# Norms by a diagonal matrix of inverse roots on TensorE, with weight and shift applied in the evictions and the residual in pieces

## The chip, the cores and the metric

The kernel runs on one core of a Trainium2 chip. The metric is the device time of one execution in microseconds (us). The core has TensorE (PE, with PEld for its weight loads), VectorE (DVE), ScalarE (ACT), GpSimd (POOL) and a queue of transfers issued by SyncE (SP). ACT and POOL issue transfers too.

## The reference, cut to what matters

Two transformer stacks follow each other, all in float32. The first has two layers on 256 rows of 1024 numbers; the second has two layers on the same rows and 256 context rows.

```
def rms_norm(x, g):            # over 1024 numbers of a row
    return x * rsqrt(mean(x*x) + 1e-6) * g
# first stack, l = 0, 1
x = x + 0.5 * swiglu_ffn(rms_norm(x, ffn1_norm[l]), ...)          # norms 0, 4
h = rms_norm(x, mix_norm[l]); u = h @ w_in[l]                     # norms 1, 5
x = x + concat(conv, pool, attention of u) @ w_out[l]
x = x + 0.5 * swiglu_ffn(rms_norm(x, ffn2_norm[l]), ...)          # norms 2, 6
x = rms_norm(x, post_norm[l])                                     # norms 3, 7
# second stack, for latent rows xl and context rows xc
h = rms_norm(x, g) * (1 + scale) + shift                          # norms 8, 9, 10, 11
x = x + gate * mixer(h);  x = x + gate * experts(h)
```

Norm 8 feeds the first mixer (Fourier and short convolution), 9 and 11 the two mixtures of 32 experts, 10 the window attention. The last mixer and mixture give latent rows only, so norm 11 has 256 rows.

## The kernel before

Rows lie in four tiles of 128 (`xres`, partitions = rows): tiles 0 and 1 are the latent rows, 2 and 3 the context rows. Norms 0 to 7 and 11 have 2 tiles, 8 to 10 have 4. All large products run in TensorE as three products of a high and a low part (`product`: hi*hi, hi*lo, lo*hi). Weights come in panels of 1 MB, read by SP into four raw slots; `split(p)` makes the high part on ACT (a cast, L1128) and the low part on DVE (L1537, helper `rest`), in three slots. Each engine runs its own list of instructions in program order; they meet at semaphores.

A norm is `norm(n)` on DVE (L1583) and ACT (L1151), `norm_T(n)` on PE (L627) and `hT_rest(n)` on DVE (L1609). After the last panel of a stage, `residual` adds the product in PSUM (the banks that TensorE writes) to `xres`, 2 tiles of 1024 columns, and only then counts `x_ready`. Half of the tiles are squared and summed on DVE (L1586), half on ACT (L1160). ACT takes the square root (L1163), DVE inverts it and refines it with one Newton step (L1565 to L1554), then multiplies each row by root and weight into `hrow` (L1603). With modulation it is root times weight times (1 + scale) (L1599), and then plus shift (L1601). PE transposes 128x128 blocks of `hrow` with the identity (L634, transpose mode), 8 blocks a tile, four to a bank. ACT casts each bank into `t_hi` (L1170), DVE writes the rest into `t_lo`. PE starts its next product when all of it is there.

Norms 3 and 7 (`post_norm`) write `xres` itself, and norm 4 or 8 follows in full. `gated_residual` (L1800) does the same as `residual` with a gate row, tile after tile. After the experts, DVE combines four tiles (L2050 to L2054), and norm 10 follows. In norms 9 and 11 the rows `hrow` also go to DRAM, where the experts' rows are gathered from; the weights of the experts are then streamed. SP loads the expert panels 4 and 5 after `row_ready`.

The order within `moe`, `even` and `odd` is written out by hand. `norm_rows(n)` on ACT issues the loads of weight, scale and shift rows, each copied over all 128 partitions; `ffn` on DVE and ACT goes through 11 units of three panels.

Of the kernel before, what the change touches and what calls it, by code (L numbers as in the profile page):

```python
# [22 lines left out]
ALU = mybir.AluOpType  # L23
# [96 lines left out]
def build(nc, A, out):  # L120
# [11 lines left out]
    with ExitStack() as ctx:  # L132
# [23 lines left out]
        eps = sb("eps", [P, 1])  # L156
        ss = sb("sum_squares", [P, 64])
# [26 lines left out]


# [25 lines left out]
        cols1 = sb("cols1", [P, DEPTH, 2 * CONV_W + 8])  # L211
# [106 lines left out]
        ms_ready = sem("mean_square_ready")  # L318
        std_ready = sem("std_ready")
# [106 lines left out]
        gain_src = []  # L426
        for l in range(DEPTH):
            gain_src += [A["ffn1_norm"][l], A["mix_norm"][l], A["ffn2_norm"][l], A["post_norm"][l]]
        for l in range(DEPTH):
            gain_src += [A["norm_mix_g_2"][l], A["norm_ffn_g_2"][l]]  # L430


        MODB = [16 * c for c in (5, 10, 15, 18)]
# [51 lines left out]
        def _(sp):  # L485
# [57 lines left out]
            def moe(m):  # L543
# [12 lines left out]
                def first_load(x, src):  # L556
                    if x < RAW:
                        sp.wait_ge(w_ready, SPLIT_PANELS[m] + x - RAW + 1)
                    else:
                        sp.wait_ge(row_ready, TILE0[10 + 2 * m])  # L560
# [56 lines left out]
        def _(pe):  # L617
# [9 lines left out]
            def norm_T(n):  # L627

                nt = NORMS[n]
                pe.wait_ge(row_ready, TILE0[n + 1])  # L630
                for j in range(2 * nt):
                    for q in range(4):
                        kk, t = (2 * j + q // 2, q % 2) if nt == 2 else (j, q)
                        mm = pe.transpose(ps[:, j, q * P:(q + 1) * P], hrow[:, t, kk * P:(kk + 1) * P], ident)  # L634
                    mm.then_inc(tr_ready, 1)

# [22 lines left out]
            def ffn(f, n):  # L659
                p0 = G0[f"ffn{f}"]  # L660
                pe.wait_ge(hT_lo, BANK0[n + 1])
                pe.wait_ge(cond_ready, 1)

                def gate_up(u, j, par, mk=None):

                    for half in range(2):
# [5 lines left out]
                        for c in range(2):  # L672
                            for kk in range(KD):
                                mm = product(ps[:, 4 + 2 * par + c, half * PC:(half + 1) * PC],
# [4 lines left out]
                def ffn_down(u, p, j, par, start=False, stop=False):  # L679
# [4 lines left out]
                    for c in range(2):  # L684
                        for t in range(2):
                            for half in range(2):
                                mm = product(ps[:, 2 * t + half, :], T(AT + (2 * par + c) * 256 + t * P, P),
                                             at(wt, slice(None), c, slice(half * BANK, (half + 1) * BANK)),
                                             start and c == 0, stop and c == 1)
# [13 lines left out]
                ffn_down(10, p0 + 32, 32, 0, stop=True)  # L703

            def mix1(l):
# [3 lines left out]
                pe.wait_ge(hT_lo, BANK0[n + 1])  # L709
# [3 lines left out]
                for b in range(2):  # L713
                    pe.wait_ge(w_ready, p + b + 1)
                    for c in range(2):
                        for kk in range(KD):
                            mm = product(ps[:, b, c * 256:(c + 1) * 256],
# [106 lines left out]
                for q in range(4):  # L824
                    rows_product(G0[f"out{l}"] + q, lambda kk, t: T(2048 + kk * 256 + t * P, P), 2,
                                 lambda t: ps[:, 2 * t + q // 2, (q % 2) * 256:(q % 2) * 256 + 256])
# [12 lines left out]
            def even():  # L839
                p = G0["even"]  # L840
                norm_T(8)
                pe.wait_ge(hT_lo, BANK0[9])
                for half in range(2):
                    rows_product(p + half, hT4, 4, lambda t: ps[:, t, half * 256:half * 256 + 256])
# [45 lines left out]
                for q in range(4):  # L890
                    rows_product(G0["even_out"] + q, lambda kk, t: T(kk * 512 + t * P, P),
                                 4, lambda t: ps[:, 2 * t + q // 2, (q % 2) * 256:(q % 2) * 256 + 256])

            def moe(m):
                nt, n = TILES[m], 9 + 2 * m
                nb, b0 = BLOCKS[m], EXPERTS * m
                norm_T(n)
                pe.wait_ge(hT_lo, BANK0[n + 1])
# [3 lines left out]
                for t in range(nt):  # L902
                    for kk in range(KD):
                        for part in range(2):
                            mm = pe.matmul(ps[:, 0, 2 * t * NLOG:2 * (t + 1) * NLOG], lhs(kk, t)[part],
                                           router_split(kk), start=kk == 0 and part == 0,
                                           stop=kk == KD - 1 and part == 1)
# [205 lines left out]
        def _(act):  # L1113
# [37 lines left out]
            def norm(n, mid=None):  # L1151
# [5 lines left out]
                if n:  # L1157
                    act.wait_ge(x_ready, n)
# [1136 lines left out]
```

## Time and profile before

| | |
|---|---|
| median of 3 runs | 2908.72 us (2908.54 to 2909.84) |
| profiled execution, its own time | 2905.86 us |
| its span, first to last instruction | 2904.0 us |
| mean granted clock of TensorE | 0.900 |
| busy: PE, PEld, DVE, ACT, POOL | 2310.4, 1590.7, 1070.7, 686.9, 117.8 us |

A busy share is an average over stages: the two expert stages (roughly 1440 to 2035 and 2310 to 2890 us) wait for transfers, the others run on PE. A timeline row gives the start, the length, the engine, line and operation, what it writes and reads, and in brackets the idle time ahead of it with what ended it.

### The profile page before, as it was taken

How to read it: one execution, taken by the hardware profiler on the slowest of the kernel's cores; microseconds unless marked ns; L12 is line 12 of the kernel's file. 1: busy time of each engine (PE TensorE's matmuls, PEld its weight loads, DVE VectorE, ACT ScalarE, POOL GpSimd, SP SyncE). 2: the span in 40 equal slices, each digit the busy share in tenths (PEclk: the TensorE clock that was granted, in tenths of full speed). 3: DMA queues.
4: the chain of work that ended last, by engine and by line, in shares of the span. 5: the costliest groups of instructions: out<-in, count | busy, mean ns of one | idle time of the engine just before them, and what ended most of it. 6: DMA issues, size and time to landing. Idle time of an engine off the chain costs nothing.

```text
span 2904.0 us, 35200 instructions
## 1 busy us (share of the span) xinstructions
PE 2310.4 (80%) x13750; PEld 1590.7 (55%) x13750; DVE 1070.7 (37%) x1570; ACT 686.9 (24%) x876; POOL 117.8 (4%) x209
## 2 busy tenths in 40 slices
PE   5998679979987699699558777877369668888885
PEld 5888478878885688587523333332355523333332
DVE  4555545555556355723420100010668410000011
ACT  3334433333335233321101000100335200000100
POOL 0001000000010000000000000000100000000000
PEclk9999789989998799899669999999679788998898
DMA  7775137757752287422149999999420269999997
GB/s 260 261 238 173 56 118 266 253 190 266 262 169 88 104 288 259 139 78 94 73 161 401 399 396 400 402 400 404 179 71 1 87 258 397 401 399 401 401 402 303
DMA packets 242628, 718.82 MB, mean 248 GB/s; under 512 B 17040, under 2 KB 156560, under 8 KB 189072
## 3 DMA queue, kind: packets, MB, share of 16 engines
q1 hardware_dynamic: 213584, 642.82, 59.7%
q10 hardware_dynamic: 19952, 48.45, 4.6%
q0 software_dynamic: 8976, 25.90, 3.0%
q8 instruction: 87, 1.43, 0.2%
q14 instruction: 29, 0.24, 0.0%
HBM read 693.70 MB, written 25.26 MB: 248 GB/s over the span
## 4 chain that ended last, share of the span: by engine, by line
PE 55%; DMA 26%; DVE 9%; issue 4%; DVEq 2%; ACT 2%; SPq 1%; ACTq 0%; POOL 0%; POOLq 0%
DMA raw<-in_w 24%; PE ps L620 13%; PE ps L621 12%; PE ps L622 12%; PE ps L934 10%; PE ps L655 2%; PE ps L634 1%; SPq L554 1%; PE ps L936 1%; PE ps L1071 1%; DVE t_lo L1537 1%; PE ps L1086 1%; DMA raw<-in_ffn_w_up 1%; DVE work L1601 1%; DMA work<-expert_rows,slot_of_token 1%
## 5 line engine op out<-in xcount | busy, mean ns | idle before, releaser
L1537 DVE TENSOR_TENSOR w_lo<-raw,w_hi 128x2048 fp32r<-128x2048 f32 x180 | 411.4, 2290 | 445.1 <-ACT w_hi L1128 445.1
L620 PE MATMUL ps<-t_hi,w_hi 128*128 128x256 f32 (+1 forms) x1568 | 456.4, 291 | 8.7 <-DVE t_lo L1537 8.6
L621 PE MATMUL ps<-t_lo,w_hi 128*128 128x256 f32 (+1 forms) x1568 | 454.1, 290 | 0.0
L622 PE MATMUL ps<-t_hi,w_lo 128*128 128x256 f32 (+1 forms) x1568 | 451.1, 288 | 0.0
L1128 ACT CAST w_hi<-raw 128x2048 fp32r<-128x2048 f32 x180 | 342.1, 1903 | 447.5 <-PE ps L622 428.5
L934 PE MATMUL ps<-raw,work 128*64 128x512 f32 x528 | 308.8, 742 | 167.0 <-DMA raw<-in_w 165.6
L2015 DVE COPY work<-ps 128x512 f32<-128x512 f32 x64 | 44.3, 692 | 932.6 <-PE ps L952 932.6
L620 PE MATMUL ps<-w_hi,t_hi 128*128 128x256 f32 (+1 forms) x1088 | 349.8, 322 | 15.3 <-DVE t_lo L1537 12.4
L622 PE MATMUL ps<-w_hi,t_lo 128*128 128x256 f32 (+1 forms) x1088 | 351.1, 323 | 0.0
L621 PE MATMUL ps<-w_lo,t_hi 128*128 128x256 f32 (+1 forms) x1088 | 351.0, 323 | 0.0
L620 PEld LDWEIGHTS ps<-t_hi,w_hi 128*128 128x128 f32 x1568 | 296.6, 189 | 30.4 <-issue 13.2
L936 PE MATMUL ps<-raw,work 128*64 128x512 f32 x528 | 310.5, 745 | 0.0
L622 PEld LDWEIGHTS ps<-t_hi,w_lo 128*128 128x128 f32 x1568 | 297.6, 190 | 4.6
L621 PEld LDWEIGHTS ps<-t_lo,w_hi 128*128 128x128 f32 x1568 | 296.1, 189 | 5.6
L934 PEld LDWEIGHTS ps<-raw,work 128*64 128x64 f32 x528 | 82.7, 167 | 371.0 <-issue 369.2
L934 PE MATMUL ps<-work 128*64 128x512 f32 x496 | 228.9, 605 | 31.9 <-DMA work<-in_w 31.9
L936 PE MATMUL ps<-work 128*64 128x512 f32 x496 | 229.4, 606 | 0.0
L620 PEld LDWEIGHTS ps<-w_hi,t_hi 128*128 128x128 f32 x1088 | 211.2, 194 | 31.7 <-DVE t_lo L1537 13.5
L952 PE MATMUL ps<-raw,work 128*64 128x512 f32 x992 | 226.7, 598 | 0.2 <-DMA raw<-in_w 0.2
L622 PEld LDWEIGHTS ps<-w_hi,t_lo 128*128 128x128 f32 x1088 | 209.5, 193 | 14.1
L621 PEld LDWEIGHTS ps<-w_lo,t_hi 128*128 128x128 f32 x1088 | 209.3, 192 | 13.5
L1394 ACT COPY work<-ps 128x512 f32<-128x512 f32 x64 | 37.5, 586 | 712.2 <-PE ps L936 712.2
(280 smaller groups left out, 2159.1 us busy)
## 6 DMA issues: line engine op xcount, KB each, us to landing
raw<-in_w SPq DMA_DIRECT2D x256, 1024.0 KB, 11.3
work<-in_w SPq DMA_DIRECT2D x128, 1024.0 KB, 10.7
work<-in_w_mod SPq DMA_DIRECT2D x32, 1536.0 KB, 6.5
raw<-in_ffn_w_gate SPq DMA_DIRECT2D x44, 1024.0 KB, 8.8
raw<-in_ffn_w_up SPq DMA_DIRECT2D x44, 1024.0 KB, 10.3
raw<-in_ffn_w_down SPq DMA_DIRECT2D x44, 1024.0 KB, 4.9
raw<-in_w_in SPq DMA_DIRECT2D x18, 1024.0 KB, 5.5
expert_rows<-work ACTq DMA_DIRECT2D x128, 128.0 KB, 7.2
```

The costliest lines, as they stand in the source:

```text
L554: sp.dma_start(expert_raw(m, x).rearrange("p (a n) -> p a n", a=1), src).then_inc(expert_landed[x], 16)
L620: pe.matmul(dst, a[0], b[0], start=start, stop=False)
L621: pe.matmul(dst, a[0], b[1], start=False, stop=False)
L622: return pe.matmul(dst, a[1], b[0], start=False, stop=stop)
L655: mm = pe.matmul(ps[32 * q:32 * q + 32, bank + a // BANK, 0:n], cond[:, kk, :], mod_raw[:, q * MOD_Q + a:q * MOD_Q + a + n], start=True, s ...
L934: first = pe.matmul(ps[0:BLK, 2 + par, :], xT[:, par, kk * BLK:(kk + 1) * BLK], w1[:, j * BANK:(j + 1) * BANK], start=kk == 0, stop=kk == ...
L936: mm = pe.matmul(ps[BLK:P, 2 + par, :], xT[:, par, kk * BLK:(kk + 1) * BLK], w3[:, j * BANK:(j + 1) * BANK], start=kk == 0, stop=kk == KD - 1)
L952: mm = pe.matmul(ps[BLK * half:BLK * half + BLK, 6 + par, :], am[:, par, c * BLK:(c + 1) * BLK], w2[:, j * D + half * BANK:j * D + (half + ...
L1128: act.copy(slot(j)[0], src).then_inc(w_hi_ready, 1)
L1394: act.copy(gusb[:, par, :], ps[:, 2 + par, :]).then_inc(gu_ready, 1)
L1537: return dve.tensor_tensor(dst, src, hi.bitcast(F32), ALU.subtract)
L2015: dve.tensor_copy(ysb[:, par, :], ps[:, 6 + par, :]).then_inc(y_copied, 1)
```

## The change

Norms are rebuilt in seven ways. (1) `norm_T` becomes a real float32 product of the raw rows with a 128x128 diagonal matrix of the inverse roots, which DVE makes from the identity (`diagonals`). (2) Weight (norms 0 to 6) or shift (8 to 11) is applied by ACT and DVE as they evict PSUM, in pieces of 128x256, from columns `gain_cols` and `shift_cols`; `shift_cols` is loaded by transfers of single 4-byte elements. For norms 8 to 11, the rows are first multiplied by weight times (1 + scale). (3) Residuals and squares go in pieces: `ffn` counts its first tile early (its last panel runs tile by tile), the mixers add quarters or halves of columns. (4) Norms 3+4 and 7+8 are merged: one root for the post norm and one for the next norm are worked out together from the sums of squares of x and of x times weight. (5) The context half of norm 8 moves into unit 9 of the last `ffn` (`context_norm`); norm 10 goes stream by stream in the combine loop, its context half is transposed after the first panel of `odd`. (6) PE waits for `t_lo` a pair of row blocks at a time (`hT_wait`). (7) The router's rows are written after `hT_rest`, and expert loads 4 and 5 wait for them.

```diff
 def norm_T(n, s=0):                                  # PE
+    pe.wait_ge(row_ready, TILE0[n] + 2 * i + 2)
-            mm = pe.transpose(ps[:, j, ...], hrow[:, t, kk * P:(kk + 1) * P], ident)
+            mm = pe.matmul(ps[:, norm_bank(n, s) + j, ...],
+                           norm_source(n)[:, t, kk * P:(kk + 1) * P], diag(n)[:, t, :], start=True, stop=True)
 def ffn(f, n):                                       # PE
-    pe.wait_ge(hT_lo, BANK0[n + 1])
+                if u == 0 and half == 0 and c == 0: hT_wait(n, kk)
-    ffn_down(10, p0 + 32, 32, 0, stop=True)
+    for t in range(2):
+        for half in range(2):
+            for c in range(2):
+                mm = product(ps[:, 2 * t + half, :], ..., False, c == 1)
+        mm.then_inc(panel_done if t else out_tile_done, 1)
 def even():                                          # PE
+    pe.wait_ge(x_part_ready, X_TILE[3][1])
+    for s in (1, 0): norm_T(8, s)
 def odd():                                           # PE
+    norm_T(10, 0)
+    pe.wait_ge(hT_lo, BANK0[10] + 4)
     for q in range(4):
+        if q == 1: norm_T(10, 1)
         rows_product(p + q, hT4, 2, ...)
+def evict(n, s=0):                                   # ACT, per bank two of
+    act.activation(t_hi[...], at, ACT.Copy, scale=gain_cols[:, n, kk:kk + 1])         # n < 8
+    act.activation(t_hi[...], at, ACT.Identity, bias=shift_cols[:, n - 8, s, kk:kk + 1])
 # ACT, ffn(3) after unit 9
+    root_table(); act.wait_ge(x_landed, 32)
+    for t in (2, 3): act.activation(..., ACT.Square, accum_out=ss[:, t:t + 1])
+    root(STEP[8, 1], 2, 2)
 def norm_rows(n):                                    # ACT
-    spread_rows(l, 3 * v, sh_rows, streams, modb_landed)
+    for s in streams:
+        act.dma_start(shift_cols[:, n - 8, s, :], mod_dram[s, a:a + D].rearrange("(k p) -> p k", p=P))
+    if n in (9, 11): spread_rows(l, 3 * v, sh_rows, streams, modb_landed)
 # ACT, moe(0) after the experts
     for s in streams:
         for t in (2 * s, 2 * s + 1): act.activation(y1, y1, ACT.Copy, scale=gates[:, 0, t:t + 1])
+        for t in (2 * s, 2 * s + 1): square(10, xres[:, t, :], 0, D, t)
+        root(STEP[10, s], 2, 2 * s)
+        if s == 1: evict(10, 0)
+def inverse_roots(step, a, c):                       # DVE
+    dve.drain().then_inc(ms_ready, 1); dve.wait_ge(std_ready, step)
+    r = 1 / std;  t = 1.5 - 0.5 * r * r * v          # four small instructions, each drained
+def diagonals(n, tiles, a=0):
+    for t in tiles:
+        dve.tensor_scalar(diag(n)[:, t, :], ident, rs[:, a + t], rt[:, a + t], ALU.mult, ALU.mult)
+def hT_rest(n, s=0):                                 # per bank two of 128x256
+    dve.scalar_tensor_tensor(t_lo[...], at, col, t_hi[...], ALU.mult if n < 8 else ALU.add, ALU.subtract)
+def after_ffn(n):                                    # norms 1, 5
+    ffn_tile(f, 0); ffn_tile(f, 1)                   # ACT squares tile 0 and half of tile 1
+    sum_squares(n, xres[:, 1, :], 0, BANK, 5)
+    inverse_roots(STEP[n], 0, 2); diagonals(n, (0, 1)); hT_rest(n)
+def after_post(n):                                   # norms 3+4, 7+8
+    for t in range(2):
+        ffn_tile(f, t)
+        dve.tensor_tensor(rows[:, t, :], xres[:, t, :], gain(n - 1), ALU.mult)
+        if n == 8: dve.tensor_tensor(hrow[:, t, :], xres[:, t, :], sc_rows[:, 0, :], ALU.mult)
+    sum_squares(n, rows[:, 1, :], 0, BANK, 7)        # ACT: x of both tiles, rows 0, half of rows 1
+    inverse_roots(step, 0, 4); diagonals(n, (0, 1), 2)
+    if n == 8: hT_rest(8, 1)
+    hT_rest(n)
+    for t in range(2): dve.tensor_scalar(xres[:, t, :], rows[:, t, :], rs, rt, ALU.mult, ALU.mult)
+def context_norm():                                  # DVE, ffn(3) between units 9 and 10
+    scale_rows(8, (0, 1)); dve.tensor_tensor(sc_rows[:, 0, :], sc_rows[:, 0, :], gain(7), ALU.mult)
+    for t in (2, 3): dve.tensor_tensor(hrow[:, t, :], xres[:, t, :], sc_rows[:, 1, :], ALU.mult)
+    inverse_roots(STEP[8, 1], 2, 2); diagonals(8, (2, 3), 0)
 # DVE, end of mix1: a quarter of the columns as each of the four panels is done
+    for q in range(4):
+        dve.wait_ge(panel_done, p + 10 + q)
+        dve.tensor_tensor(x, ps[:, 2 * q:2 * q + 2, 0:256], x, ALU.add)
+        if q == 2: split(p + 14)
+def gated_residual_4(first_panel):   # norm 9: first 512 columns of 4 tiles two panels before the end,
+    ...                              # then per tile mult, add, times scale, on 512 columns
+def gated_residual_2(first_panel):   # norm 11: quarters of 256 columns of 2 tiles
+    ...
 # DVE, moe: after hT_rest
+    for t in range(nt):
+        dve.scalar_tensor_tensor(hrow[:, t, :], hrow[:, t, :], rs, sh_rows[:, t // 2, :], ALU.mult, ALU.add).then_inc(rows_ready, 1)
 # DVE, moe(0): combine(0), combine(1), then norm 10 of stream 0; combine(2), combine(3), then of stream 1
+    scale_rows(10, (s,)); two products with hrow; inverse_roots(STEP[10, s], 2 * s, 2); diagonals(10, ...)
```

## Rows read from the trace of the kernel before

**Rows 1.** Groups by line, shapes apart: the transposes (busy, mean, idle before)

```profile
L634 PE MATMUL ps<-consts,work 128*128 128x128 f32 x208 | 41.3, 385 | 198.4 <-DVE work L1601 120.3 <-DVE work L1603 78.1
```

**Rows 2.** Timeline of DVE and PE in norm 1

```profile
236.04 2.35 DVE L1621 SCALAR_TENSOR_TENSOR x_rows<-ps,x_rows 128x1024 f32<-128x1024 f32 x2 [1.27 <-PE ps L622]
238.55 1.23 DVE L1586 CUSTOM_DVE_ANT_0 work<-x_rows 128x1024 f32<-128x1024 f32 x1 [0.16 <-issue]
...
240.26 0.17 DVE L1565 TENSOR_SCALAR variance<-sum_squares 128x2 f32<-128x2 f32 x1 [0.47 <-ACT std L1163]
...
241.54 2.48 DVE L1603 SCALAR_TENSOR_TENSOR work<-x_rows,rstd,work 128x1024 f32<-128x1024 f32 x2
...
244.07 3.43 PE L634 MATMUL ps<-consts,work 128*128 128x128 f32 x16 [8.07 <-DVE work L1603]
248.90 0.38 PE L620 MATMUL ps<-t_hi,w_hi 128*128 128x256 f32 x1 [1.40 <-DVE t_lo L1537]
```

**Rows 3.** Timeline of PE at norms 0, 2, 4, 8, 9 and 11

```profile
30.68 3.65 PE L634 MATMUL ps<-consts,work 128*128 128x128 f32 x16 [30.68 <-DVE work L1603]
35.73 0.58 PE L620 MATMUL ps<-t_hi,w_hi 128*128 128x256 f32 x1 [1.40 <-DVE t_lo L1537]
...
404.82 3.27 PE L634 MATMUL ps<-consts,work 128*128 128x128 f32 x16 [8.06 <-DVE work L1603]
...
623.79 3.68 PE L634 MATMUL ps<-consts,work 128*128 128x128 f32 x16 [15.18 <-DVE work L1603]
628.87 0.58 PE L620 MATMUL ps<-t_hi,w_hi 128*128 128x256 f32 x1 [1.40 <-DVE t_lo L1537]
...
1226.69 5.38 PE L634 MATMUL ps<-consts,work 128*128 128x128 f32 x32 [24.37 <-DVE work L1601]
1234.12 0.39 PE L620 MATMUL ps<-w_hi,t_hi 128*128 128x256 f32 x1 [2.05 <-DVE t_lo L1537]
...
1426.89 5.96 PE L634 MATMUL ps<-consts,work 128*128 128x128 f32 x32 [27.41 <-DVE work L1601]
1434.62 0.30 PE L905 MATMUL ps<-t_hi 128*128 128x72 f32 x1 [1.77 <-DVE t_lo L1537]
...
2303.66 3.67 PE L634 MATMUL ps<-consts,work 128*128 128x128 f32 x16 [15.40 <-DVE work L1601]
2308.74 0.43 PE L905 MATMUL ps<-t_hi 128*128 128x72 f32 x1 [1.40 <-DVE t_lo L1537]
```

**Rows 4.** Timeline of DVE and PE at norm 10

```profile
2047.41 1.28 DVE L2050 SCALAR_TENSOR_TENSOR work<-work,gates 128x1024 f32<-128x1024 f32 x1 [7.80 <-ACT work L1459]
...
2087.51 0.38 PE L620 MATMUL ps<-w_hi,t_hi 128*128 128x256 f32 x1 [2.04 <-DVE t_lo L1537]
```

**Rows 5.** Timeline of PE: transposes and float32 products of the attention

```profile
310.26 1.04 PE L756 MATMUL ps<-consts,work 128*128 128x128 f32 x8
...
362.79 1.22 PE L795 MATMUL ps<-work 128*128 128x128 f32 x4 [0.46 <-ACT work L1255]
...
920.79 0.71 PE L795 MATMUL ps<-work 128*128 128x128 f32 x4 [0.46 <-ACT work L1255]
```

**Rows 6.** Groups by line: pieces of 128x256 read from PSUM (mean ns)

```profile
L1558 DVE SCALAR_TENSOR_TENSOR work<-work,ps 128x256 f32<-128x256 f32 x64 | 27.0, 421 | 60.1 <-ACT work L1402 60.1
...
L1234 ACT ACTIVATE work<-ps,cols 128x256 f32<-128x256 f32 x4 | 1.7, 487 | 0.0
```

**Rows 7.** Windows in norm 1: window, length, busy of five engines, PEclk, DMA, GB/s

```profile
240.40:244.00 3.60, 0.00 (x0) 0.00 (x0) 3.20 (x9) 1.53 (x1) 0.00 (x0) 0.50 0.00 0
247.20:248.80 1.60, 0.30 (x3) 0.07 (x1) 1.47 (x3) 0.91 (x2) 0.00 (x0) 1.00 0.67 184
```

**Rows 8.** The line of ACT's loads: issue ns, first and last start

```profile
L1115 ACTq DMA_DIRECT2D work<-in_norm_ffn_g x2: 334/336/339, 1350.5 to 2259.1; - x2
...
L1115 ACTq DMA_DIRECT2D work<-in_cond_cols x1: 677/677/677, 2.0 to 2.0; - x1
```

**Rows 9.** Transfers by line: count, KB each, median us from issue to landing

```profile
work<-in_cond_cols ACTq DMA_DIRECT2D x1, 8.0 KB, 10.7
```

More of the change, by code:

```diff
@@ L901, in moe @@
                 pe.wait_ge(router_lo, m + 1)
[L902 to L907, printed above, removed]
+                for s in streams_of(n):
+                    pe.wait_ge(hT_lo, BANK0[n] + 4 * s + 4)
+                    for t in (2 * s, 2 * s + 1):
+                        for kk in range(KD):
+                            for part in range(2):
+                                mm = pe.matmul(ps[:, 0, 2 * t * NLOG:2 * (t + 1) * NLOG], lhs(kk, t)[part],
+                                               router_split(kk), start=kk == 0 and part == 0,
+                                               stop=kk == KD - 1 and part == 1)
                 mm.then_inc(logit_ready, 1)
@@ L1290, in mix1 @@
                 split(p + 13)
+                split(p + 14)
             def load_taps(l):
@@ L1319, in _ @@
                 mix1(l)
-                norm(4 * l + 2, mid=G0[f"ffn{2 * l + 1}"] + 1)
+                norm(4 * l + 2)
                 if l == 1:
@@ L1327, in _ @@
                 ffn(2 * l + 1)
-                norm(4 * l + 3)
             def even():
                 p = G0["even"]
-                norm(8, mid=p + 2)
+                after_post(8)
+                root(STEP[8, 0], 4)
+                evict(8, 1)
+                evict(8, 0)
+                split(p + 2)
                 act.wait_ge(tr_ready, BANK0[9])
@@ L1376, in moe @@
                 a.then_inc(router_hi, 1)
+                root_table()
+                act.wait_ge(x_part_ready, X_COLUMNS[n])
+                first = 512 if m == 0 else 768
+                for t in range(nt):
+                    square(n, xres[:, t, :], 0, first, t)
+                for t in range(nt):
+                    act.wait_ge(x_part_ready, X_COLUMNS[n] + (t if m == 0 else 0) + 1)
+                    sq = square(n, xres[:, t, :], first, D, 4 + t)
+                sq.then_inc(sums_ready, 1)
                 act.wait_ge(x_ready, 9 + 2 * m)
                 spread_rows(m, 5, g_rows, streams, gate_landed)
-                norm(n)
+                root(STEP[n], nt)
+                for s in streams:
+                    evict(n, s)
                 for t in range(nt):
+                    act.wait_ge(rows_ready, TILES[0] * m + t + 1)
                     load(h_dram[t * P:(t + 1) * P, :], hrow[:, t, :], h_stored)
@@ L1464, in odd @@
                 spread_rows(1, 2, g_rows, (0,), gate_landed)
-                norm(10, mid=p + 2)
+                evict(10, 1)
+                split(p + 2)
                 act.wait_ge(row_ready, TILE0[11])
@@ L2081, in odd @@
                 p = G0["odd"]
-                norm(10, 4, modulated=True)
-                hT_rest(10, mid=p + 2)
+                for s in range(2):
+                    hT_rest(10, s)
+                split(p + 2)
                 for x in (3, 4, 5, 6, 7):
```

475 lines of the change are left out of this document (357 added, 118 removed).

## Prediction

> **What bounds the kernel now.** I read the groups by line first, for what TensorE waits for. Ahead of the 208 transposes of the norms it is idle for 198.4 us in all, ended always by the DVE line that has written the normalised row [rows 1]. Then I read the timeline at each norm. In norm 1 PE stops at 236.00 (244.07 less 8.07), DVE adds two tiles (2.35), squares, goes through small operations on 128x2, writes two rows (2.48), PE transposes, and its next product starts at 248.90 [rows 2]: 12.9 us from stop to product. Norms 2, 5 and 6 have the same idle time, 8.06, and the same steps [rows 2, 3]. By the same subtraction norm 3 with 4 takes 20.3 us (608.61 to 628.87), 7 with 8 takes 31.8 (1202.32 to 1234.12), 9 takes 35.1 (1399.48 to 1434.62), 11 takes 20.5 (2288.26 to 2308.74), and norm 0 starts its product at 35.73 [rows 3]. In norm 10 it is 40.1 us from the first combining operation to the product [rows 4]. No other work is queued on PE in these stretches and the weights wait ready, so each microsecond cut out of one moves all that follows. That also holds ahead of the experts, although they are bound by transfers: their stream stands still until the router has made its table, and starts earlier with it.
>
> **Prices.** A transpose costs 0.11 us at the high clock ((1.04-0.27)/7, eight in the row, 0.27 being the tail of the last) [rows 5] and 0.215 at the low one (3.65 for 16, less a tail of 0.42) [rows 3]. The diagonal product is float32 by float32, 128x128 by 128. The attention's value product has just this form: 16 products appear there as 32 instructions in each layer, two for each product. Four instructions take 0.71 us, so with the same tail of 0.27 one is 0.145, at most; the first of them is stretched by its start, so I take one instruction to cost what a transpose costs, 0.11, and a product 0.22, with 0.29 as the other end. At the low clock the row of 1.22 for four gives 0.27 an instruction or 0.53 a product as the upper end; I take twice the transpose, 0.43 [rows 3, 5]. Sixteen products then take 3.5 us at the high and 6.9 at the low clock, against 1.8 and 3.4 for transposes. This is the change's cost: 208 products, +23 us at the high clock.
>
> The granted clock had fallen to 0.50 in norm 1 by 240.40, after some 4 us without work, and stood at 1.00 at 247.20, ahead of the next real product, after 3 us of transposes [rows 2, 7]. With the change the idle time is 4 to 7 us. I assume one low stretch of about 3.4 us in each norm, in which 8 products run instead of 15: +1.6 us each; none at all is the lower end, the low clock throughout the upper.
>
> The Trainium skill, "TensorE: Matmul & The Clock Gate", section Terms, says that transpose mode is 4 times faster for float32. By that rule a product would cost 0.44 rather than 0.22, and the sum below would lose 46 us more; the rows of the attention speak for 2. I keep this as a rival.
>
> PE no longer waits for the last bank. ACT takes 2 x 0.49 for a bank and DVE 2 x 0.42 [rows 6], against PE's 0.88, and the first product needs the last bank only after 18 matmuls (2.1 us), so evictions are covered; without that cover the old tail of 1.4 us [rows 2] comes back in each norm.
>
> The chain of small steps, called R below: variance 0.25, root on ACT and back 0.5 (0.47 in the row), four drained operations 1.0, two diagonals 0.45; from 240.26 to 241.54 five of these take 1.28 [rows 2]. No row shows a diagonal; one lies between 0.17, a small operation, and 0.42, a 128x256 piece [rows 2, 6], and I take 0.22. R is 2.2 us, 2.0 to 2.6. It takes the place of 2.48 for two rows, or of four pairs of multiplication and addition.
>
> **Norm by norm**, from PE's stop to its next product.
> - Norms 1 and 5: tile 0 is added before the stop. After it: tile 1 1.25, the half squares and the handover 1.0, R 2.2, products 3.5+1.6: 9.6, against 12.9. Gain 3.3 each, 6.6.
> - Norms 2 and 6: only the last quarter is left, 0.7, two 256-column sums 0.9, R 2.2, 3.5+1.6: 8.9. Gain 4.0 each, 8.0. The split of panel 1 moves ahead of the norm, behind the last panel's 5.6 us of products.
> - Norms 3+4: DVE is busy with a split until about 1.2 us before the stop, then four operations of 1.2 on 1024 columns end 3.7 after it, squares 0.9, two more small steps 0.5, R 2.2, products 5.1: 12.4, against 20.3. The product of before started at the low clock (0.58 against 0.38 in the other norms [rows 2, 3]), worth 1.9 more. Gain 9.8.
> - Norms 7+8: the context half is done by the last unit of the ffn. There DVE gets about 8.5 us more (three times 1.2 for the scales, two rows 2.5, small steps) and ACT two table loads and two squares, and `ffn`'s last unit has about 7 us to spare, so PE stops 1.5 later. After the old stop DVE has six operations of 1.2 (11 us with a split that is now late by 1.5 and the squares), R 2.2 and 16 products 3.5: 14.4 against 31.8, the context's 16 products lying under DVE's work. Gain 17.4.
> - Norm 9: only the last tile's half is left, 2.0 with its 0.5 of handover, ACT's half square 0.9, R 2.2, 32 products 7.1+1.6: 13.8, against 35.1. Gain 21.3. The router's rows (4 x 1.28) lie under the router's 13 us of products. Loads 4 and 5 of the experts' panels start about as late as before, with 30 us and more to spare.
> - Norm 10: combining and scaling stay on DVE (16.0, 2.4, 4 x 1.2 and two chains), and the eviction of stream 0 waits for stream 1's root on ACT: product at 31.3 after the first combining operation, against 40.1, but PE starts at the low clock (2.5) and the context's 16 products (3.5) now lie behind the first panel. Gain 2.8.
> - Norm 11: 2.0, two squares 1.2, R 2.2, products 5.1: 10.5, against 20.5, less 0.5 for issuing the column transfer ahead of the casts that PE waits for (0.33 to 0.68 [rows 8]). Gain 9.5.
> - Norm 0: two rows of 1.25 make room for diagonals (2.0), the products cost 3.5 more, the tail of 1.4 goes, and the product that follows runs at the high clock sooner: gain 1.5, with 0 to 3.
>
> Sum: 6.6 + 8.0 + 9.8 + 17.4 + 21.3 + 2.8 + 9.5 + 1.5 = 77 us. The profiled execution took 2905.9 (its span and 1.9 around it), 2.9 below the median of the runs. 2905.9 - 77 = 2829, and on the scale of the median 2832. What a measurement of this kernel can tell from no change is about 0.2%, 6 us.
>
> **Rivals.**
> - *Better clock* (8%): the shorter idle times leave the clock high, and the router starts at it. Nine low stretches of 1.6 fall away, and some 5 us in two routers: 2812. For it: idle times near 4 us are at the edge of what made it fall in norm 1. Against: there it had fallen at just that time.
> - *Low clock throughout* (10%): the products run mostly at the low clock, 0.43 for 0.22: 208 x 0.21 less the nine stretches already counted, +30: 2862. Against: transposes alone raised it [rows 7].
> - *Float32 products cost four times a transpose* (4%), the skill's rule above: 208 x 0.22 more, 2878. Against: the value products [rows 5].
> - *The expert stages give their gain back* (4%): norms 9 and 11 gain 31 us, but the gather or a load that now waits for the router's rows is as late as before: 2863. Against: the table, not a load, is last there.
> - *Slower* (2%): the column transfers of 1024 single elements land late, and DVE stands at `scale_rows` in norms 9, 10 and 11. The nearest row, 1024 pieces of 8 bytes, landed in 10.7 us, in the crowd of the first loads [rows 9]. They are issued at about 1351, 2033 and 2260 and wanted some 26, 22 and 10 us later, on DVE with 18 us of slack in the last: nothing is lost below 22 us, and the kernel is slower than before only from about 50 us each. The Trainium skill, "DMA: Bandwidth & Descriptors", section Rules for kernel authors, says that a non-contiguous last dimension becomes one descriptor per element, and to rearrange it; by itself it gives no time.
>
> **Numbers.** The forecast has 72%, the rivals 8, 10, 4, 4 and 2. The unknown prices move the forecast by -16 (no low stretch) to +15 (0.29 a product). The range 2814 to 2860 holds the forecast with its bounds and leaves out the far rivals. Faster 0.97, same 0.01, slower 0.02.
>
> **What would show it.** In the trace after, idle time ahead of the diagonal products should fall from 198 to about 90 us, with DVE `diagonals` as releaser; they should be 416 instructions at 0.11 or 0.21 apart. The clock should show one short low stretch per norm instead of two or more. PE should go from the diagonal products to the next product without a wait. Just ahead of the last ffn panel there should be a stall of 1 to 2 us, and DVE should never stand at `scale_rows`. The prediction is wrong if the products are further apart, if the merged norms wait for ACT's four squares longer than 1 us, or if `odd`'s third panel comes late behind the context's eviction.

## The result, and the profile after

The changed kernel takes 2837.01 us (median of 4 runs, 2835.73 to 2839.40), beside 2908.63 for the kernel before (2908.03 to 2909.84): a ratio of 0.9754, 95% interval 0.9737 to 0.9771. That is 71.6 us less; 77 were forecast. The profiled execution took 2835.73 us, its span is 2833.9 and its mean granted clock 0.905. The transposes of [rows 1] have turned into these two groups by line (busy, mean ns, idle before and its releaser):

```profile
L674 PE MATMUL ps<-work 128*128 128x128 f32 x256 | 40.2, 332 | 56.0 <-DVE work L1773 52.8 <-DVE x_rows L1794 3.2
L674 PE MATMUL ps<-work,x_rows 128*128 128x128 f32 x160 | 27.9, 355 | 44.9 <-DVE work L1773 44.9
```

They are 416 instructions for 208 products, busy for 68.1 us where the transposes took 41.3, and PE's idle time ahead of them is 100.9 us (56.0 and 44.9), where it was 198.4. L1773 is `diagonals`. The timeline of DVE in norm 1 answers to [rows 2] (start, duration, line, operation, idle before):

```profile
231.60 2.57 DVE L1794 SCALAR_TENSOR_TENSOR x_rows<-ps,x_rows 128x1024 f32<-128x1024 f32 x2
234.40 0.69 DVE L1753 CUSTOM_DVE_ANT_0 work<-x_rows 128x512 f32<-128x512 f32 x1 [0.23 <-issue]
...
235.71 0.17 DVE L1761 RECIPROCAL rstd<-std 128x2 f32<-128x2 f32 x1 [0.30 <-ACT std L1239]
...
236.67 0.60 DVE L1773 TENSOR_SCALAR work<-consts,rstd,rstd_error 128x128 f32<-128x128 f32 x2
```

and PE's, at the same place:

```profile
232.51 0.40 PE L662 MATMUL ps<-w_hi,t_lo 128*128 128x512 f32 x1
237.32 5.47 PE L674 MATMUL ps<-work,x_rows 128*128 128x128 f32 x32 [4.41 <-DVE work L1773]
242.54 0.36 PE L660 MATMUL ps<-t_hi,w_hi 128*128 128x256 f32 x1
```

Tile 0 is added before the last product ends, half a tile is squared, and two diagonals of 0.30 us each stand where two rows took 2.48. The next real product follows the diagonal ones without a wait: 9.6 us from stop (232.91) to product (242.54), where there were 12.9. The other norms, to be read beside [rows 3]; the number in brackets is PE's idle time:

```profile
394.50 1.41 PE L674 MATMUL ps<-work,x_rows 128*128 128x128 f32 x6 [3.83 <-DVE work L1773]
605.63 1.22 PE L674 MATMUL ps<-work 128*128 128x128 f32 x4 [7.03 <-DVE work L1773]
1187.43 0.80 PE L674 MATMUL ps<-work 128*128 128x128 f32 x2 [3.24 <-DVE x_rows L1794]
1367.95 1.44 PE L674 MATMUL ps<-work 128*128 128x128 f32 x5 [5.11 <-DVE work L1773]
2229.90 1.01 PE L674 MATMUL ps<-work 128*128 128x128 f32 x3 [4.83 <-DVE work L1773]
2237.89 0.30 PE L980 MATMUL ps<-t_hi 128*128 128x72 f32 x1 [1.93 <-DVE t_lo L1784]
```

From PE's stop to its next product, read from the trace at every norm, and what each place gave with the stretch of products ahead of it:

| norm | before | after | forecast gain | gain there | stretch ahead of it |
|---|---|---|---|---|---|
| 0 | 35.7 | 34.0 | 1.5 | 1.7 | - |
| 1, 5 | 12.9, 13.1 | 9.6, 9.6 | 3.3 each | 3.3, 3.5 | 1.4 and 1.8 shorter |
| 2, 6 | 12.9, 12.9 | 9.1, 9.3 | 4.0 each | 3.8, 3.6 | 0.3 and 0.1 longer |
| 4 | 20.3 | 12.6 | 9.8 | 7.7 | 0.1 shorter |
| 8 | 31.8 | 13.3 | 17.4 | 18.5 | **8.2 longer** (198.95 to 207.18) |
| 9 | 35.1 | 13.7 | 21.3 | 21.4 | unchanged |
| 10 | 60.5 | 52.7 | 2.8 | 7.8, less 3.5 for stream 1's products later | 2.2 shorter |
| 11 | 20.5 | 12.8 | 9.5 | 7.7 | 1.4 longer besides |

From norm 11's product to the end it is 0.7 us more (596.0 from 595.3). The idle times came out as forecast almost everywhere. The largest miss is the stretch ahead of norm 8, in ffn(3), where nothing was expected but 1.5 us. The timeline of ACT and its queue just after norm 6 shows it:

```profile
977.68 0.73 ACTq L1193 DMA_DIRECT2D x_rows<-in_ctx  x1
978.44 0.49 ACTq L1193 DMA_DIRECT2D work<-in_norm_mix_g  x1
978.96 1.10 ACTq L1193 DMA_DIRECT2D work<-mod_rows  x2
980.09 5.28 ACTq L1449 DMA_DIRECT2D shift_cols<-mod_rows  x2
985.39 3.82 ACTq L1193 DMA_DIRECT2D work<-mod_rows  x2
989.31 1.90 ACT L1206 CAST w_hi<-raw 128x2048 fp32r<-128x2048 f32 x1 [11.18 <-PE ps L662]
```

Two `shift_cols` loads take 5.28 us to issue, the next two loads 3.82, and the cast that ffn(3)'s next panel wants comes behind all of them. PE's timeline:

```profile
988.28 0.28 PE L662 MATMUL ps<-t_hi,w_lo 128*128 128x256 f32 x1
993.59 0.58 PE L660 MATMUL ps<-t_hi,w_hi 128*128 128x256 f32 x1 [5.03 <-DVE w_lo L1705]
```

PE sits idle for 5.0 us. Its row names DVE's w_lo, but DVE waited for ACT's cast, and the cast for the queue: a releaser is only the last link. The view of line L1449, which issues the `shift_cols` loads, gives the issue in ns (least, median, most) and the landing in us:

```profile
L1449 ACTq DMA_DIRECT2D shift_cols<-mod_rows x7: 456/731/4568, 980.1 to 2196.2; - x7
...
  DVE work L1868: 4.6, 1
...
DMA to landing us min/median/max: 4.8/8.5/24.9
```

Five of the seven issues took 0.5 to 1.2 us; the other two, each the second of a pair, 4.0 behind norm 6 and 4.6 ahead of norm 10. The longest landing, 24.9, holds DVE for 4.6 us at norm 10, ahead of `scale_rows`:

```profile
1991.06 1.23 DVE L2373 TENSOR_TENSOR x_rows<-x_rows,work 128x1024 f32<-128x1024 f32 x1
1996.93 1.23 DVE L1868 SCALAR_TENSOR_TENSOR work<-work 128x1024 f32<-128x1024 f32 x1 [4.64 <-DMA shift_cols<-mod_rows]
```

### The profile page after: what moved, and what is told of

The parts are those of the page before. It is cut to its first block, busy times and chain, and to the rows that moved or that the text cites. A ratio compares the mean times of both kernels' runs of the same rounds, so it can differ in the third digit from the quotient of the medians.

```text
span 2833.9 us, 35797 instructions
## 1 busy us (share of the span) xinstructions
PE 2350.8 (83%) x13958; PEld 1617.6 (57%) x13958; DVE 1057.4 (37%) x1634; ACT 718.1 (25%) x969; POOL 118.3 (4%) x209
## 4 chain that ended last, share of the span: by engine, by line
PE 57%; DMA 26%; DVE 7%; issue 3%; ACT 2%; DVEq 2%; SPq 1%; ACTq 1%; POOL 0%; POOLq 0%
DMA raw<-in_w 24%; PE ps L660 13%; PE ps L661 12%; PE ps L662 12%; PE ps L1009 11%; PE ps L674 2%; PE ps L701 2%; DMA shift_cols<-mod_rows 1%; SPq L594 1%; PE ps L1011 1%; DVE w_lo L1705 1%; PE ps L1149 1%; PE ps L1164 1%; DMA raw<-in_ffn_w_up 1%; DMA router_rows<-work 1%
## 5 line engine op out<-in xcount | busy, mean ns | idle before, releaser
L1009 PE MATMUL ps<-raw,work 128*64 128x512 f32 x528 | 330.9, 787 | 163.3 <-DMA raw<-in_w 161.9
L660 PE MATMUL ps<-w_hi,t_hi 128*128 128x256 f32 (+1 forms) x1088 | 350.8, 322 | 23.9 <-DVE t_lo L1784 11.5
L1011 PE MATMUL ps<-raw,work 128*64 128x512 f32 x528 | 332.4, 790 | 0.0
L1009 PE MATMUL ps<-work 128*64 128x512 f32 x496 | 229.2, 605 | 17.3 <-DMA work<-in_w 17.2
L1027 PE MATMUL ps<-raw,work 128*64 128x512 f32 x992 | 226.7, 598 | 0.2 <-DMA raw<-in_w 0.2
```

Source lines behind the costliest of these rows:

```text
L660: pe.matmul(dst, a[0], b[0], start=start, stop=False)
L1009: first = pe.matmul(ps[0:BLK, 2 + par, :], xT[:, par, kk * BLK:(kk + 1) * BLK], w1[:, j * BANK:(j + 1) * BANK], start=kk == 0, stop=kk == ...
L1011: mm = pe.matmul(ps[BLK:P, 2 + par, :], xT[:, par, kk * BLK:(kk + 1) * BLK], w3[:, j * BANK:(j + 1) * BANK], start=kk == 0, stop=kk == KD - 1)
L1027: mm = pe.matmul(ps[BLK * half:BLK * half + BLK, 6 + par, :], am[:, par, c * BLK:(c + 1) * BLK], w2[:, j * D + half * BANK:j * D + (half + ...
```

## The experiments

Theory: the gain is the work taken from behind PE's stops, place by place as in the forecast; what is short of it is due to the loads of single elements. Rivals: the stretch ahead of norm 8 lost its time to `context_norm`; the diagonal product itself carries (or costs) the difference; the clock does. Each kernel below is the changed one with one edit (e8 and e11 with several), timed in 5 rounds. There were three occasions, each on another chip: e1 to e4, e5 to e8, and e9 to e11; the kernel before took 2911.17, 2909.79 and 2907.71 us beside them. The changed kernel was timed again on the second alone (e5, 2834.45 us); differences are taken from that or from the 2837.01 of the first comparison, and across occasions they carry 2 to 3 us of their own.

**Loads of shift_cols moved to POOL's queue (e1).** The loop at L1448 goes; POOL gets

```
mod_store(1)
+ shift_columns((8, 9))        # the same transfers, then_inc(shift_landed, 16)
...
mod_store(3)
+ shift_columns((10, 11))
# ACT, in evict(n, s):
+ if n >= 8: act.wait_ge(shift_landed, 64 if n < 10 else 112)
- MODB = [16 * c for c in (5, 12, 17, 21)]
+ MODB = [16 * c for c in (3, 8, 11, 14)]
```

> The seven shift_cols loads leave ACT's queue: POOL issues those of norms 8 and 9 once the second quarter of the modulation rows is stored, those of norms 10 and 11 after the fourth, with a semaphore of their own. Nothing is left out. Theory 1 (the loads of single elements cost what the prediction did not count: 5.3 us of a stalled PE in ffn(3), 4.6 us of DVE before norm 10, 0.6 us before norm 11): 2837.0 - 10.5 = 2826.5 us, the segment from norm 6 to norm 8 down from 207.2 to about 202, scale_rows of norm 10 no longer waits. Theory 2 (those 8.2 us come from context_norm and from the other loads on the same queue): within 5 us of 2837. Theory 3 (the transfers just get in the way of others wherever they are issued): no gain, 2837 or more.

Measured: 2823.24 us (2821.23 to 2825.58), ratio 0.9700, interval 0.9687 to 0.9713: 11 to 14 us less. The stretch ahead of norm 8 is 199.8 us, ACT's cast comes 4.8 us after the start of norm 6's product instead of 12.3, and DVE no longer waits at norm 10:

```profile
980.29 2.40 ACTq L1194 DMA_DIRECT2D work<-mod_rows  x4
982.79 1.91 ACT L1207 CAST w_hi<-raw 128x2048 fp32r<-128x2048 f32 x1 [3.65 <-issue]
```

Of the 7.4 us that come back ahead of norm 8, 5.0 are PE's idle time; the rest goes with the clock. These two windows (window, length, busy of PE, PEld, DVE, ACT and POOL, granted clock, DMA share, GB/s) are of the changed kernel, then of e1:

```profile
960.00:1010.00 50.00, 40.79 (x302) 39.91 (x301) 24.26 (x36) 19.11 (x23) 0.00 (x0) 0.90 0.65 224
960.00:1010.00 50.00, 45.81 (x352) 44.40 (x351) 29.67 (x39) 21.05 (x24) 0.00 (x0) 0.97 0.70 252
```

In the changed kernel the granted clock is at its low level once more for 6.8 us from 992.1 on, just behind the stall; in e1 it stays high there. Of the 4.6 us at norm 10 only 2.5 come back (stop to product 50.2 from 52.7), since the experts' rows that the first weighting needs landed 2 us later after the stop in this execution. On POOL an issue takes 0.91 us, all seven alike, and nothing there waits. Theories 2 and 3 are out.

**The same loads from contiguous memory (e2).**

```
- mod_dram[s, a:a + D].rearrange("(k p) -> p k", p=P)
+ A["gain_cols"][:, n - 8, :]
```

This leaves out the right shifts: the result is wrong and the experts get other rows, so only the places ahead of norm 9 compare strictly.

> The same seven loads at the same place on ACT's queue, but each reads 32 contiguous bytes a partition (from gain_cols, so the shifts have other values) in place of 1024 single elements. Theory 1 (the element pieces hold the queue and land late): as much gain as moving them, about 2826.5 us, with issues of 0.5 us. If it is the number of issues ahead of ACT's next cast that matters: no change, 2837 us.

Measured: 2825.77 us (2822.99 to 2826.91), ratio 0.9705, interval 0.9692 to 0.9719: 9 to 11 us less with the loads left where they are. The two issues in ffn(3) still take 2.4 us together, more than forecast, but the cast comes 6.9 us after norm 6's product, and the stretch ahead of norm 8 is 199.6 us, as in e1. The stretch ahead of norm 11 is 5.4 us longer than in the changed kernel, with the granted clock low for 23.9 us of it instead of 13.7; why is open. So seven loads at this place cost nothing there if their pieces are 32 bytes, and by e1 single elements cost nothing on a queue where nothing waits: it takes both, single elements and work behind them.

**context_norm's rows on POOL (e3).**

```
# DVE, context_norm:
- scale_rows(8, (0, 1)); sc_rows[0] *= gain(7); hrow[2:4] = xres[2:4] * sc_rows[1]
+ dve.wait_ge(context_rows, 3)
# POOL, ahead of mod_store(3): the same operations
```

> The rows of context_norm (two rows scaled for norm 8, one by the second gain, two context tiles times their row: about 7 operations of 128x1024) move from DVE, ahead of the last unit of ffn(3), to POOL some 100 us earlier; DVE keeps roots and diagonals. Nothing is left out. Theory (DVE's 5.9 us there make PE wait 1.0 us for activations and the first residual tile of norm 8 start late): 2 to 3 us less, about 2834.5 us, if POOL's own work beside DVE costs nothing. Rival (DVE had the room, or POOL's 128x1024 operations slow DVE): 2837 us or more.

Measured: 2827.92 us (2825.35 to 2830.86), ratio 0.9711, interval 0.9698 to 0.9724: 6.5 to 9 us less. But the stretch ahead of norm 8 is only 0.7 us shorter (206.4), and norm 8 itself gives 0.4; stretch and norm together take 219.3 us, against 220.5 in the trace of the changed kernel and 219.2 in its second (e5). So `context_norm` costs at most about 1 us, as little as forecast, and most of this gain lay elsewhere: from norm 9's product to the end of the experts 584.5 us instead of 590.2, a stage that the edit does not touch. What it was, e9 tells.

**Rows scaled on DVE, PE transposes, at norms 0, 1, 2, 5, 6 (e4).**

```
- diag(n)[:, t, :] = ident * rs * rt        # two of 128x128
+ hrow[:, t, :] = xres[:, t, :] * rs * rt   # two of 128x1024
- pe.matmul(ps.., xres block, diag(n)[:, t, :])
+ pe.transpose(ps.., hrow block, ident)
```

> Norms 0, 1, 2, 5 and 6 alone: DVE multiplies the two row tiles by their roots (2 x 0.81 us in place of two diagonals of 0.60 us together) and PE transposes them with the identity (0.11 us each in place of 0.21 for a float32 product at the high clock); weights, eviction and waits by pairs stay. Theory (the gain at these norms is from pieces, waits and fused evictions, the diagonal gives next to nothing): +1.0 us on DVE, about -1 us until PE's first banks are full, each of five norms: 2837 us, within 4. Rival (the diagonal itself carries the gain, as less work on DVE): 2837 + 5 x 2 = 2847 us. Rival (the float32 product is the dear part, four times a transpose): 2837 - 5 x 2 = 2827 us.

Measured: 2835.36 us (2832.45 to 2838.28), ratio 0.9741, interval 0.9727 to 0.9754: no difference from the changed kernel. At norm 1, PE and DVE:

```profile
237.11 3.67 PE L675 MATMUL ps<-consts,work 128*128 128x128 f32 x16 [5.35 <-DVE work L1778]
```

```profile
235.52 1.54 DVE L1778 TENSOR_SCALAR work<-x_rows,rstd,rstd_error 128x1024 f32<-128x1024 f32 x2
```

The rows take 0.94 us more than the diagonals, PE's sixteen transposes 1.8 us less than the products. ACT's last eviction ends 9.9 us after the stop, with diagonals 10.8. From stop to product it is 0.8 to 1.3 us less at each of norms 1, 2, 5 and 6, but the stretch between norms 1 and 2 is 2.5 longer, with more time at the low clock in the attention. Up to norm 6's product the traces of e4, e8 and e11 take 974.4 to 975.7 us, and the seven of kernels whose code is the changed one's up to there 975.5 to 978.0: the diagonal gives nothing at these norms and costs 2 us at most, which the whole time doesn't resolve. A product costs two transposes, not four.

**The changed kernel again (e5).**

> The changed kernel itself once more, beside the other runs of this call, as the baseline for differences of a few us: ratio to the kernel before 0.9754, within 0.001. If it comes out near 0.972, much of what the earlier experiments seemed to gain is a matter of the occasion; if it stays, moving context_norm's rows did gain 9 us where only 1 us is seen at its place.

Measured: 2834.45 us (2832.91 to 2836.68), ratio 0.9742, interval 0.9728 to 0.9755. The occasion accounts for 2.6 us in time, 0.0012 in the ratio; e3's interval lies wholly below this one.

**The product waits for all eight pieces (e6).**

```
- if kk % 2 == 0: pe.wait_ge(hT_lo, ... + kk // 2 + 1)
+ if kk == 0:     pe.wait_ge(hT_lo, ... + 4)
```

> The product after norms 0, 1, 2, 4, 5, 6 (and stream 0 of norm 8) waits for all eight evicted pieces, in place of pairs. Nothing is left out. Theory: the last pair is ready 3 x 0.96 us after the first; by pairs PE has done three quarters of the first 24 products (2.6 us at 0.11 each) by then, so waiting for all costs 2.0 us a norm, six norms: 12 us more than the changed kernel, about 2849 us. Rival (the pairs arrive as slowly as PE would go anyway, or the clock rises as late either way): under 4 us, 2841 us.

Measured: 2851.04 us (2849.52 to 2851.56), ratio 0.9795, interval 0.9782 to 0.9809: 16.6 us more than e5. From stop to product it is 2.2 us more in norms 1, 2 and 5, as forecast, 2.7 and 3.2 in norms 4 and 6, and the stretches of products behind norms 1 and 4 are 1.5 longer each. Norms 0 to 6 come to 14 us in this way. The stretch ahead of norm 8 is 4 us shorter, since the wait behind norm 6 now covers most of the stall in ffn(3); and 3 us of the 16.6 lie in the first stage of the experts, which the edit doesn't touch. The timeline of PE at norm 1 shows the wait, and instructions 0.21 apart behind it, at the low clock (0.11 to 0.12 in the changed kernel there):

```profile
245.96 0.45 PE L660 MATMUL ps<-t_hi,w_hi 128*128 128x256 f32 x1 [1.93 <-DVE t_lo L1784]
246.20 0.42 PE L661 MATMUL ps<-t_lo,w_hi 128*128 128x256 f32 x1
246.42 0.41 PE L662 MATMUL ps<-t_hi,w_lo 128*128 128x256 f32 x1
```

**Tile 0's residual after the last product (e7).**

```
- if t == 0: dve.wait_ge(out_tile_done, f + 1)
- else:      dve.wait_ge(panel_done, G0[f"ffn{f}"] + 33)
+ dve.wait_ge(panel_done, G0[f"ffn{f}"] + 33)
```

> The first residual tile after each of the four blocks ffn waits for the last product, as it did before the change; the rest stays. Nothing is left out. Theory: tile 0's 1.22 us (norms 1 and 5), 2.45 us (norm 4) and 1.7 us (norm 8, where DVE is late anyway) then lie behind the stop: 6.6 us more than the changed kernel, about 2843.6 us. Rival (ACT's squares, not DVE, end the chain): under 2 us.

Measured: 2842.71 us (2837.32 to 2843.11), ratio 0.9761, interval 0.9748 to 0.9775: 8.3 us more than e5. In norm 1 the idle time grows by 1.3 us:

```profile
238.32 2.08 PE L674 MATMUL ps<-work,x_rows 128*128 128x128 f32 x8 [5.72 <-DVE work L1773]
```

but stop to product by 2.3 (11.9), since the products behind it take 6.2 us in place of 5.2: the low stretch is longer. It is longer at norms 2 and 6 as well (stop to product 10.0 and 10.2), where the idle time is as before, and the stretches of products in between are 1.1 to 1.2 shorter. From norm 0's product to norm 2's, 1.3 us more of idle time come to 2.1 in all; at norm 4, 1.4 come to 1.1. In norm 4 the wait grows by 1.4 and not by 2.45, since DVE was busy with a split until 1.2 us before the stop, as the forecast has it, and only that much of tile 0's work lay ahead. The idle times of the four norms grow by 5.8 us together. 4.3 of the 8.3 us lie in the first stage of the experts, which the edit doesn't touch; up to the stop ahead of norm 9 this trace is 6.2 us behind e5's and 2.8 behind the first of the changed kernel.

**Shift on POOL, context rows on POOL, router by pairs, e4's rows (e8).** The edits of e1, e3 and e4, and in the router

```
- pe.wait_ge(hT_lo, BANK0[n] + 4 * s + 4)
+ if t % 2 == 0: hT_wait(n, kk, s)
```

> The changed kernel with shift_cols on POOL's queue, context_norm's rows on POOL, the router's products waiting by pairs, and rows scaled on DVE with PE transposes at norms 0, 1, 2, 5 and 6. Nothing is left out. By the places: 13.8 us measured for the first, 1 to 2 for the second where it is seen (9 if its whole measured difference holds), 2 at norm 11 for the third, 0.5 to 0.9 at each of five norms for the fourth: 2837.0 - 20 = 2817 us. Rival (each of the first experiments gained by the same better occasion, not by its edit): no better than the first alone, 2823 us.

Measured: 2817.16 us (2816.18 to 2819.73), ratio 0.9682, interval 0.9669 to 0.9695. Norm 11 goes from 12.8 to 11.0 us. That the forecast is met so closely is in part luck: it counted 20 us from 2837.0, e5 on the same occasion is 17.3 us away, and some 4 of these are POOL's gap, which e9 takes up and the forecast did not hold.

**One early copy on POOL (e9).** In the changed kernel the timeline of POOL at the first gather reads

```profile
1411.63 0.18 POOL L2508 COPY token_of_slot_col<-token_of_slot 64x1 uint32<-64x1 uint32 x1 [252.22 <-DVEq L2313]
1417.99 0.96 POOL L2510 DMA_INDIRECT work<-router_rows,token_of_slot_col  x1 [6.18 <-issue]
```

(from e5, whose code is the same). The edit:

```
+ pool.memset(table_col[0:BLK, :], 0); pool.drain()
+ pool.tensor_copy(table_col[0:BLK, 0:1], table_col[0:BLK, 1:2]); pool.drain()
  mod_store(3)
```

> The changed kernel with one memset and one copy of a 64x1 column on POOL some 300 us before the router, and nothing else. In the changed kernel's trace 6.18 us pass between POOL's first copy of a slot column and the issue of the first gather of expert rows, in the second router stage 1.43 us; in the trace of the third experiment, whose POOL had computed before, 1.29 us, and the 4 us that it gained beyond its own place lie there. Theory (the first compute operation of its kind on POOL costs some 5 us, whenever it comes): those 6.18 us become about 1.3, 4 to 5 us less in all, about 2830.5 us. Rival (the gap has to do with the router stage or its DMA, not with a first use): no change, 2834.5 to 2837 us.

Measured: 2828.62 us (2828.01 to 2830.49), ratio 0.9730, interval 0.9716 to 0.9743: 5.8 us less than e5, or 3.8 if each is taken from the kernel before beside it (the two intervals overlap), and

```profile
1411.44 0.18 POOL L2508 COPY token_of_slot_col<-token_of_slot 64x1 uint32<-64x1 uint32 x1 [251.98 <-DVEq L2313]
1412.90 0.96 POOL L2510 DMA_INDIRECT work<-router_rows,token_of_slot_col  x1 [1.28 <-issue]
```

6.18 us have become 1.28, and norm 9's product to the experts' end is 583.5 us. That accounts for 4.9 us of e3's gain that its place did not explain. In e3, 5.07 us lie between POOL's first two operations on rows and its next one, off PE's path. In e9, 8.9 us lie between the memset and the copy; which of the two pays is open. The kernel before had the same 6.19 us there, so the change neither made nor mended it.

**Norm 9's residual after the panels (e10).**

```
- dve.wait_ge(panel_done, first_panel + 2)
+ dve.wait_ge(panel_done, first_panel + 4)
```

> The gated residual ahead of norm 9 starts after the last product, as one block of work, in place of pieces ahead of it; the rest stays. Nothing is left out. DVE's work ahead of the stop is 7.4 us for columns 0 to 511 and 3 x 2.3 us for three tiles. Theory (those pieces are the bulk of norm 9's gain): 14.2 us more behind the stop, about 2849.5 us. Rival (the gain came from merged evictions and diagonals, and ACT's squares or the clock take up the difference): 7 us more or less, about 2842 us.

Measured: 2849.18 us (2846.97 to 2851.94), ratio 0.9801, interval 0.9788 to 0.9815: 14.7 us more than e5 (16.8 if each is taken from the kernel before beside it). PE's idle time ahead of norm 9:

```profile
1380.17 2.08 PE L674 MATMUL ps<-work 128*128 128x128 f32 x8 [18.95 <-DVE work L1773]
```

18.95 instead of 5.11, 13.8 us more at the place. So pieces make two thirds of norm 9's 21.4 us; the other 7 (35.1 before, 28.5 here) are, by subtraction alone, rows no longer written and evictions no longer waited for.

**The combined kernel with norm 10 by pairs (e11).** `evict(10, 0)` moves ahead of stream 1's squares, and the first product of `odd` calls `hT_wait(10, kk)`.

> The combined kernel (2817.2 us) and, at norm 10, ACT evicts stream 0 while it waits for stream 1's rows, and the first product waits by pairs. Nothing is left out. Theory: three pairs of 0.96 us no longer lie ahead of the product, 2 to 2.5 us less, about 2815 us. Rival (ACT's evictions delay the squares and the root of stream 1, which bound the panel after): 2817 us or more.

Measured: 2815.46 us (2813.27 to 2816.93), ratio 0.9682, interval 0.9668 to 0.9695: not told apart from e8. At its place it gave what was expected (from the first diagonal product to the first real one 14.6 us, 16.9 in e8), but PE's idle time ahead of it was 0.9 longer in that execution, and the rest is within the spread. This and e8 are the fastest kernels of the study, about 17 us below the changed one, each taken from the kernel before beside it.

## Why the prediction was right, and where it was off

- **The mechanism and the sum** hold: 71.6 us for 77, the likeliest case. The forecast 2832.0 lies 5.0 below the result, and the terms of norms 1, 2, 5, 6, 8 and 9 are within 1.1 us where they stand. e10, e7 and e6 put three of the edits back one at a time and lose 14.7, 8.3 and 16.6 us; up to norm 9's product their traces show about 14, 3 to 6 and 12 to 15, near the 14.2, 6.6 and 12 worked out from rows. That the sum is so close is in part luck: the stretch ahead of norm 8 lost 8.2 us where 1.5 was put down, and stretches where nothing was forecast gave 5.4 (1.4, 1.8 and 2.2, ahead of norms 1, 5 and 10, the last within what that stage varies by itself). Two of the signs named for being wrong did not show: in the merged norms ACT's squares end before DVE's, and `odd` never waits for the context's eviction.
- **The diagonal product's price** was right: 0.111 us at the high and 0.213 at the low clock for an instruction, two instructions each, against 0.110 and 0.213 for a transpose in one. The rival that it costs four transposes is out, by the groups after and by e4. In the Trainium skill, "TensorE: Matmul & The Clock Gate", section Terms, transpose mode is 4 times faster for float32; the trace disagrees, since at equal clock a product takes two instructions of the length of one transpose.
- **The two diagonals** took 0.60 us, not 0.45; small.
- **The clock** did as assumed, one low stretch a norm: in norm 1 the window of the diagonal products has a granted clock of 0.67, and the product that follows starts at the high one. Neither clock rival came. The forecast had expected two or more low stretches a norm before the change; in norm 1 there was one before as after, of 6.8 us and then 3.4. It did not foresee the low stretch behind the stall in ffn(3).
- **The step that failed** is the price of the column transfers. It was taken as 0.33 to 0.68 us of issue, from [rows 8], and as free below a landing of 22 us, from [rows 9], and only at norms 9, 10 and 11. For five of the seven the issue was near that, 0.5 to 1.2 us. The place that it missed is the first two, behind norm 6: there they held the queue for 5.28 us and the loads behind them for 3.82, PE sat idle for 5.0 and then ran at the low clock. At norm 10 one landed in 24.9 us, and the sentence that DVE never stands at `scale_rows` is wrong by 4.6 us. The rows chosen as nearest priced one such load with two others ahead of it on the queue, and nothing of what stood behind it. A row of the trace before hints at that: the load right behind the 1024 pieces took 2.69 us to issue, where the two others of its kind (`work<-in_consts`) took 0.34. It is a hint and no more, since one plain load later in that first crowd took 2.68 as well:

```profile
2.68 2.69 ACTq L1115 DMA_DIRECT2D work<-in_consts  x1
```

  e1 and e2 show the cause; the size is 11 to 14 us by e1, 9 to 11 by e2. The rival named for it had the mechanism, and its 22 us were near the 20 after which DVE wanted the second load at norm 10, but it took the landing of [rows 9] for typical and lacked the place behind norm 6. The Trainium skill, "DMA: Bandwidth & Descriptors", section Rules for kernel authors, warns of one descriptor per element. The runs agree that this is dear where work stands behind (8.5 us of landing as the median, 24.9 at most, on ACT's queue), and e1 that it is cheap where none does (0.91 us of issue, 7.4 at most to land).
- **Norms 4 and 11** gave 2.1 and 1.8 less at their places. At norm 11 it is one wait: the router's products wait for all four pairs, 1.93 us, which the forecast had read as pairs; e8 takes it back (12.8 to 11.0). Norm 4's missing 2.1 is mostly the 1.9 put down for the clock, which came in the next stretch (200.69 to 198.91), so its sum holds.
- **Norm 8's sum** does not add up as written: 11 and 2.2 and 3.5 are 16.7, not 14.4. It comes out if the 11 us hold R, as they do in the trace (from the stop to the second diagonal 8.9 us, and the stop 1.5 later).
- **Norm 10** was forecast as 8.8 from the first combining operation to the product, less 2.5 and 3.5: net 2.8. It gave 5.0 there (35.1 from 40.1), since DVE waited 4.6 for the column transfer, and 2.8 ahead of the first combining operation, where none was forecast; the stretch up to norm 11 is 4.9 longer, which nets 2.9. The two misses cancel, by luck; only the landing was tested.
- **context_norm** left PE idle for 0.6 us where 1 to 2 was forecast; e3 finds 0.7 in the stretch.
- **Not tested:** the merging of norms 3+4 and 7+8. Their places gave 7.7 and 18.5 us, a third of the whole, and no kernel puts it back; that it is the merging, and for norm 8 the context half done early, rests on the sum from rows alone. The same holds for most of norm 11's 7.7.
- **Not settled:** why the first stage of the experts (norm 9's product to their end) takes 583 to 586 us in e3, e8, e9 and e11, where POOL's gap is gone, but anything from 587 to 592.5 in the others, which have the same gap.

## What to carry to other kernels

Price each new transfer by its number of pieces and by what stands behind it on its queue, at every place where it is issued, and give transfers of single elements a queue on which nothing waits; that would have been worth 11 to 14 us here, nearly as much as norm 9's pieces. When rows are to be normalised behind a long product, cut the residual so that all but the last piece lies ahead of the stop, and let the first product start on the first evicted pair; whether the scaling is a diagonal on PE or a row operation on DVE mattered by 2 us at most over five norms. When an edit gains more than its place shows, look for the surplus by segments and test it alone.

## What the runs showed of the hardware

- A load of 1024 single 4-byte elements took up to 4.57 us to issue on ACT's queue and 24.9 to land, with its median at 0.73 and 8.5; the ones of 128 pieces of 32 bytes issued in 0.45 (1.7 at most), and the same 1024 elements issued by POOL in 0.91 every time, landing in 7.4 at most (e1). The load of whole rows behind two such ones took 3.3 us to issue, the next 0.5 again.
- Behind POOL's first copy of a slot column 6.18 us passed to the next issue, in the second router stage 1.43. Operations on rows (e3, 1.29) or a memset and a 64x1 copy (e9, 1.28) hundreds of us earlier took some 5 us out of the way. The four memsets at the start of the program do not: every kernel has them.
- POOL took 2.4 to 3.5 us for a 128x1024 operation that DVE did in 1.2; in e3 that cost PE nothing, since the stretch did not get longer.
- In e7 1.3 us more of PE's idle time came to 2.1 over norms 1 and 2 together, and 1.4 to 1.1 at norm 4. Where the granted clock was low moved between traces of the same code: norm 9's stop to product was 13.7 to 15.0 us at an idle time of 5.1.
